# Cached key pages loaded as whole rows and turned in pairs, and the first overflow block gathered between the last scatters, in a decoder step on one core

## What is computed

```python
def _forgetting_attention(q, k, v, fq, fk, q_off):
    ...
        s = jnp.einsum('bqhd,bkhd->bhqk', q[:, a:b], k[:, :nk], ...) * scale
        s = s + fq[...] - fk[...]
        p = jax.nn.softmax(jnp.where(mask, s, -jnp.inf), axis=-1)
        outs.append(jnp.einsum('bhqk,bkhd->bqhd', p, v[:, :nk], ...))
```

## Time and profile before

| | |
|---|---|
| runs | 2081.64, 2071.94, 2058.39 us; median 2071.94 |
| profiled execution | 2073.77 us |
| its span, first to last instruction | 2072.2 us |
| mean granted TensorE clock | 0.939 of full speed |
| PE, PEld, DVE, ACT, POOL busy | 1680.5, 1021.7, 686.2, 310.0, 355.0 us |
| moved by DMA | 674.14 MB, mean 325 GB/s |
| attention groups 0 to 15 | 1165.94 to 1381.07 us of the span |
| overflow block, gather to scatter | 966.73 to 982.72 us |

### The profile page before, as it was taken

One profiled execution on the slowest core, in us unless ns is written; L12 is line 12 of the kernel. 1 busy time (PEld: TensorE's weight loads), 2 busy tenths in 40 slices (PEclk: granted clock), 3 DMA queues, 4 the chain that ended last, 5 costly groups with the idle time before them and its releaser, 6 DMA issues. The chain is left out here.

```text
span 2072.2 us, 34016 instructions
## 1 busy us (share of the span) xinstructions
PE 1680.5 (81%) x13065; PEld 1021.7 (49%) x13066; DVE 686.2 (33%) x1821; ACT 310.0 (15%) x665; POOL 355.0 (17%) x453
## 2 busy tenths in 40 slices
PE   5997989497788987876699988887587889987775
PEld 3455654354455554443455666654354555543432
DVE  0211235611412432221631266547312333331126
ACT  0221211110001111010011244331010011110000
POOL 3000100122211222221001012200122122222210
PEclk8999999699999999997799999998699999999997
DMA  9479883699999999993942599995599999999966
GB/s 334 144 286 339 299 322 102 277 418 422 423 388 380 412 421 409 405 404 145 355 137 81 189 299 333 328 337 195 199 423 423 415 418 406 421 418 407 411 259 228
DMA packets 132060, 674.14 MB, mean 325 GB/s; under 512 B 28111, under 2 KB 40527, under 8 KB 91620
## 3 DMA queue, kind: packets, MB, share of 16 engines
q1 hardware_dynamic: 84880, 570.20, 69.6%
q10 hardware_dynamic: 21604, 55.96, 8.0%
q0 software_dynamic: 25456, 46.27, 6.2%
HBM read 651.03 MB, written 46.94 MB: 337 GB/s over the span
## 5 line engine op out<-in xcount | busy, mean ns | idle before, releaser
L2331 PE MATMUL bank<-ring,work 128*64 128x256 f32 x4096 | 481.8, 388 | 107.1 <-DMA ring<-in_exp_w 104.1
L2331 PEld LDWEIGHTS bank<-ring,work 128*64 128x64 f32 x4096 | 327.4, 140 | 297.7 <-issue 118.5
L2343 PE MATMUL bank<-ring,work 128*64 128x512 f32 x1032 | 251.6, 605 | 63.8 <-DVE work L1768 60.4
L813 POOL DMA_INDIRECT work<-u_d,work x128 | 130.6, 1020 | 781.0 <-DVE work L1736 427.2
L2059 PE MATMUL bank<-ring,uT 128*128 128x512 f32 (+1 forms) x896 | 257.1, 503 | 7.1 <-DVE u L1489 4.2
L1736 DVE COPY work<-work 128x1 int32<-128x1 int32 (+1 forms) x128 | 19.3, 153 | 656.9 <-ACT work L1188 656.1
L2059 PEld LDWEIGHTS bank<-ring,uT 128*128 128x128 f32 (+1 forms) x896 | 119.1, 169 | 136.0 <-issue 114.4
L820 POOL DMA_INDIRECT pair_d<-work x128 | 132.4, 1034 | 124.9 <-issue 73.9
L2343 PEld LDWEIGHTS bank<-ring,work 128*64 128x64 f32 x1032 | 73.9, 136 | 151.7 <-issue 146.6
L1182 ACT COPY work<-bank 128x512 f32<-128x512 f32 x128 | 75.0, 586 | 368.0 <-PE bank L2343 364.6
L1188 ACT ACTIVATE work<-bank 128x128 f32<-128x128 f32 x128 | 35.5, 277 | 531.9 <-PE bank L2331 531.9
(11 more groups left out here) (363 smaller groups left out, 1706.9 us busy)
## 6 DMA issues: line engine op xcount, KB each, us to landing
ring<-in_exp_w SPq DMA_DIRECT2D x128, 2048.0 KB
ring<-in_exp_w SPq DMA_DIRECT2D x128, 1024.0 KB
ring<-in_ada_w SPq DMA_DIRECT2D x24, 2048.0 KB, 12.9
ring<-in_cache_k SPq DMA_DIRECT2D x128, 256.0 KB, 6.4
ring<-in_cache_v SPq DMA_DIRECT2D x128, 256.0 KB, 6.9
ring<-in_gla_w_in SPq DMA_DIRECT2D x6, 2048.0 KB, 15.0
ring<-in_kv_w_mod SPq DMA_DIRECT2D x4, 2048.0 KB, 10.1
work<-pair_d ACTq DMA_DIRECT2D x4, 2048.0 KB, 9.6
```

The costliest lines, as they stand in the source:

```text
L813: pool.indirect_dma_start(out=xg[:, s, :], out_offset=None, in_=u_d, in_offset=bass.IndirectOffsetOnAxis(ap=xi[:, s:s + 1], axis=0), bound ...
L2331: ins = mm(psum[s][64 * c:64 * c + 64, 0:2 * P].rearrange("p (a n) -> p a n", a=2), xT[:, s, j * P + 64 * half:j * P + 64 * half + 64], gu ...
L2343: ins = mm(psum[3 + s][64 * c:64 * c + 64, :], hT[:, s, 64 * f:64 * f + 64], w[:, f, c * 512:(c + 1) * 512], start=(f == 0), stop=(f == 1) ...
```

## The change

Four edits are made together.

1. Keys are loaded as whole rows: one transfer of 128 rows of 4 KB for each page, eight for a sequence instead of sixteen of 2 KB rows, all ahead of its two value halves. Page j is issued when the odd group of the sequence before has turned its page j; both groups of a sequence read the same place, and TensorE waits for a landing only in the even group. Units 6 and 7 belong to pages 4 to 7, both halves.
2. TensorE turns and scores pages two at a time. ScalarE's copy of page 4 moves behind the copies of the turned probabilities, that of page 6 behind the prompt's; VectorE makes the prompt's diagonal ahead of its copy of page 5.
3. The overflow block's gate and up products use the common `gate_up`: 256 columns at a time from the two units where before a loop wrote 128.
4. GpSimd's look-up and gather for overflow block 0 is issued between the scatters of experts 61 and 62; for block j + 1 it is done after block j's results have landed.

The core of the diff:

```diff
-        def key_page(half, j):
-            return ring_pair(4 + 2 * half)[:, j, :]
+        def key_page(j):
+            return ring[:, 4 + j // 2, (j % 2) * D:(j % 2 + 1) * D]
...
-                wr.take(("fox_k", half), 2, (kt_full, 8 * GROUPS - 8 + 8 * half), loads=0)
+                wr.take(("fox_k", half), 2, (kt_full, 8 * GROUPS - 4 + 4 * half), loads=0)
...
+                for j in range(PAGES):
+                    if not first:
+                        sp.wait_ge(kt_full, b * 16 + (j - 7))
+                    elif j % 4 == 0:
+                        free_units(("fox_k", j // 4))
+                    sp.dma_start(key_page(j), W["cache_k"][ds(page[j], 1)].rearrange("o r h d -> (o r) (h d)"))\
+                      .then_inc(sem(f"k_landed{j}"), 16)
                 for half in range(2):
-                    if first:
-                        free_units(("fox_k", half))
-                    for j in range(PAGES):
-                        if not first:
-                            sp.wait_ge(kt_full, b * 16 + (8 * half + j - 15))
-                        rows = W["cache_k"][ds(page[j], 1)].rearrange("o r h d -> (o r) (h d)")
-                        sp.dma_start(key_page(half, j), rows[:, half * 512:(half + 1) * 512])\
-                          .then_inc(sem(f"k_landed{half}{j}"), 16)
                     if first:
                         free_units(("fox_v", half))
...
                 for e in range(60, 64):
                     one(e, e % 3, last=(e >= 61))
+                    if e == 62:
+                        wait(pool, "over_placed", l + 1)
+                        pool.wait_ge(sem("xT_full"), NE * l + NE - 2)
+                        pool.wait_ge(sem("y_stored1"), 16 * Y_STORED[l][1])
+                        gather_over(l, 0)
                 pool.wait_ge(sem("yi_ready"), base + NE)
                 scatter(0, sem("y_stored0"))
...
+            def gather_over(l, j):
                 done = sem(f"pool_over{l}")
+                col = pool.value_load(ov_idx[0:1, ds(j, 1)], min_val=0, max_val=1023)
+                with pool.If(col < 512):
...
                     pool.wait_ge(sem(f"over_stored{l}"), j * 16 + 16)
+                    gather_over(l, j + 1)
...
                 keys_turned(g, 2)
                 if g:
                     exponents(g - 1)
-                keys_turned(g, 4)
                 prompt_exponents(g)
                 if g:
                     probs_turned(g - 1)
+                keys_turned(g, 4)
+                prompt_turned(g)
                 keys_turned(g, 6)
-                prompt_turned(g)
                 prompt_out(g)
...
+                prompt_norm(g)
                 keys_turned(g, 5)
-                prompt_norm(g)
...
+                    gate_up(1, ring[:, 3:5, :].rearrange("p a (k n) -> p k a n", n=FE), done)
...
             def turn_keys(g, j):
                 b, s = divmod(g, 2)
-                pe.wait_ge(sem(f"k_landed{s}{j}"), 16 * (b + 1))
+                if s == 0:
+                    pe.wait_ge(sem(f"k_landed{j}"), 16 * (b + 1))
...
+                turn_keys(g, 3)
                 page_scores(g, 0)
-                turn_keys(g, 3)
                 page_scores(g, 1)
-                turn_keys(g, 4)
-                page_scores(g, 2)
                 new_scores(g)
                 if g:
                     turn_probs(g - 1)
+                turn_keys(g, 4)
                 turn_keys(g, 5)
+                page_scores(g, 2)
                 page_scores(g, 3)
                 prompt_turn(g)
                 turn_keys(g, 6)
+                turn_keys(g, 7)
                 page_scores(g, 4)
-                turn_keys(g, 7)
                 page_scores(g, 5)
```

More of the change, by code:

```diff
@@ L347, in hybrid_trunk_step @@
         sh_down = ln
-        ov_gate, ov_up = (ring[:, n, :].rearrange("p (h m) -> p h m", h=2) for n in (3, 4))
         ov_down = ring[:, 5, :].rearrange("p (f n) -> p f n", f=2)
@@ L849, in experts @@
                     one(e, e % 3, last=(e >= 61))
+                    if e == 62:
[3 more added lines that the diff above has]
+                        gather_over(l, 0)
                 pool.wait_ge(sem("yi_ready"), base + NE)
                 scatter(0, sem("y_stored0"))
-            def overflow(l):
+            def gather_over(l, j):
                 done = sem(f"pool_over{l}")
-                wait(pool, "over_placed", l + 1)
-                pool.wait_ge(sem("xT_full"), NE * l + NE - 2)
-                pool.wait_ge(sem("y_stored1"), 16 * Y_STORED[l][1])
-                def body(j):
+                col = pool.value_load(ov_idx[0:1, ds(j, 1)], min_val=0, max_val=1023)
+                with pool.If(col < 512):
                     col = pool.value_load(ov_idx[0:1, ds(j, 1)], min_val=0, max_val=BLOCKS * NE - 1)
@@ L869, in body, with overflow @@
                         bounds_check=2 * TOK - 1, oob_is_err=False).then_inc(sem(f"over_xg{l}"), 16)
+                    pool.nop()
+                with pool.Else():
+                    pool.nop()
+            def overflow(l):
+                def body(j):
                     pool.wait_ge(sem(f"act_over{l}"), j * 2 + 2)
@@ L2403, in body @@
                     pe.wait_ge(sem(f"over_w{l}"), j * 16 + 16)
-                    for kk in range(KT):
-                        half, jj = divmod(kk, 4)
-                        for c in range(2):
-                            for a, w in enumerate((ov_gate, ov_up)):
-                                ins = mm(psum[1][64 * c:64 * c + 64, a * P:(a + 1) * P],
-                                         xT[:, 1, jj * P + 64 * half:jj * P + 64 * half + 64],
-                                         w.rearrange("p a (k n) -> p (a k) n", n=FE)
-                                         [:, kk, c * P:(c + 1) * P], start=(kk == 0 and a == 0),
-                                         stop=(kk == KT - 1), skip_group_check=True)
-                    ins.then_inc(done, 1)
+                    gate_up(1, ring[:, 3:5, :].rearrange("p a (k n) -> p k a n", n=FE), done)
                     pe.wait_ge(sem(f"over_dve{l}"), j * 3 + 2)
@@ L2545, in turn_keys @@
                     ins = pe.transpose(psum[j % 2][:, i * P:(i + 1) * P],
-                                       key_page(s, j)[:, i * P:(i + 1) * P], ident[:, :])
+                                       key_page(j)[:, (4 * s + i) * P:(4 * s + i + 1) * P], ident[:, :])
                 ins.then_inc(kt_full, 1)
```

## The result

The kernel after takes 2081.46 us (median of 20 runs), the kernel before 2072.61 (20 runs): a ratio of 1.006, 95% interval 1.004 to 1.0081. The change costs about 9 us; the forecast was 2060, and 2081.46 lies at the upper end of its range, on the other side of no change. The profiled execution of the kernel after happened to be one of its short ones, 2065.5 us; at the end of expert 62's down product, ahead of everything that the edits change for TensorE, it is already 8.8 us ahead of the profiled execution of before (940.91 against 949.68). So the comparison is made by stretches, each from its own first row, and a second profile of the kernel after (e12, an execution of 2072.3 us) stands beside the first.

A forecast was written before the change was run, and what follows sets the result against it. The chain to the end bounds: attention stage, output product, overflow block, with transfers and TensorE nearly equal. 4.4 + 2 + 6 = 12.4 gained from 2073.77 or the median 2071.94 gives 2061.4 or 2059.5; predicted 2060, range 2041 to 2082.

The forecast's parts named there:

- Alternation and the order: TensorE, attention stage: turning and scoring pages in twos saves 0.6 us a group; groups 0 to 3 gain 4.4 us.
- The pair of 23.84: Attention stage: two groups without key waits, followed row by row, take 23.84 us in place of 26.15, good to 0.8.
- a round trip: TensorE switching between transposes and scores and back costs about 0.19 to 0.2 us; 3 fewer a group.
- the wait for the diagonal: Attention stage: the 0.82 us wait ahead of the prompt's transposes in a group, claimed to go.
- Keys: Key loads, groups 4 to 15: a pair between 24.4 and 28.3 us, taken as 27.2, as now; no gain.
- The working by landing times: Even groups from group 4: page 7 lands 12.2 us in, is wanted at 7.7, so 4.5 us of wait.
- The pair of 28.3: Attention stage from group 4: an even group of 16.2 us makes the pair 28.3, 1.1 more than now.
- Rival B: Key waits in six even groups lower TensorE's clock: 1.1 + 2.7 us a pair, 12.4 slower, 2086; chance 0.11.
- theory S: Experiments' theory, not the prediction's: with whole-row keys a loop runs in series through SP, landing and even group.
- Output product: Product behind the attention stage: its 2.03 us wait for first weights goes; 2 us gained, bounds 0 and 4.7.
- Overflow: Overflow block, first expert layer: early gather lets TensorE turn rows 6.6 us earlier; 6 gained, bounds 0 and 8.5.
- rival C: Overflow block: the gather is early and brings nothing because something else holds the block, 2066; chance 0.12.

The follow-up runs named there:

- e12: The kernel after, unchanged, run once more for a second profile: 2072.3 us, one run.
- e11: Kernel after with the keys of sequence 0 loaded once and used for all sequences, other key loads left out: 2036.5 us, one run.
- e4: Kernel after with the next sequence's page numbers read early, behind the first value half: 2068.1 us, ratio to before 0.997 to 1.0033.
- e10: e4 with ten places for key pages in place of eight, two pages loaded ahead of the second value half: 2052.0 us, ratio 0.9828 to 0.9931.
- e1: Kernel before with the new order on TensorE, ScalarE and VectorE alone, keys still in halves: 2058.7 us, ratio 0.9912 to 0.9988.
- e2: Kernel before with the whole-row key loads alone, old order on the engines: 2088.9 us, ratio 1.0074 to 1.0139.
- e6: Kernel after with each key page loaded by two transfers of 2 KB rows: 2090.4 us, ratio to before 1.0049 to 1.0112.
- e3: Kernel before with the overflow edits alone (early gather, 256-column gate and up): 2073.4 us, ratio 1.002 (0.9993 to 1.0048).
- e8: e3 with the scatter's index copy put off, so the gather need not wait for expert 61's scatter: 2066.7 us, ratio 0.9973 (0.9935 to 1.001).
- e14: e3 with the 32 KB load in_kv_w_rest issued in the middle of the first expert loop: 2061.5 us, ratio to before 0.9914 to 0.9973.
- e15: Kernel before with the 32 KB load in_kv_w_rest issued in the middle of the first expert loop, nothing else: 2066.8 us, ratio 0.9942 to 0.9999.
- e7: e1 with the page numbers read early, keys in halves: 2050.1 us, ratio to before 0.9881 to 0.9955.
- e9: Kernel before with new order, page numbers read early, keys in halves, and early gather with late scatter index copy: 2059.6 us, ratio 0.9938 (0.9912 to 0.9964).
- e13: e9 with the 32 KB load in_kv_w_rest issued in the middle of the first expert loop: 2044.9 us, ratio to before 0.987 (0.9832 to 0.9908).

## Why the prediction was wrong

- **Alternation and the order: right, and a little low.** The pair of 23.84 by the chain is 23.60 in the trace after and in e11, a round trip 0.27 us where 0.19 to 0.2 was read, and the wait for the diagonal is gone. Groups 0 to 3 take 46.1 us after (a key wait of 0.99 at the end included) and 45.0 in e11, where 47.7 was forecast. They gain more because the 52.14 were not undisturbed: group 0 had the longest wait for the diagonal (1.7) and the lower clock behind it, and goes from 12.68 to 9.40.
- **Keys: the step that failed** is "a pair longer than that leaves the DMA idle, shortens the queue ahead of the next keys, and so shortens the wait again". The DMA did go idle (share 0.90 in the stage after, 0.96 before), and nothing was shortened, because the next keys are not asked for sooner when the DMA is idle: SP stands behind the values product and the page numbers (e4 gives 1.6 us a pair back), and whole-row places come free in odd groups alone (e10 gives 1.9 more). 27.2 was taken between 24.4 and 28.3; it is 29.9 and 30.4, over both bounds. The working by landing times had held: it gave 4.5 us of wait in an even group and none in odd ones, and measured are 27.0 in six even groups, 4.5 each. The pair of 28.3 that came of it was given up for the middle of the two, and what lies beyond it shows on TensorE as busy time at the lower clock, which the forecast put at nothing.
- **Rival B is what was seen**, with a chance of 0.11: key waits in even groups, and the granted clock at 0.50 behind them. Its price was 1.1 + 2.7 a pair; measured against before it is 2.8 a pair. Against e1, which has the same order at a mean clock of 0.98, the kernel after loses 18.8 us in the stage, 9.1 of busy time, which goes with the lower clock (0.92), and 9.7 of waits. I had both halves and put the clock's at little, because the waits are short one by one. That the stage would be 9 us shorter at the full clock is not shown: no run has the waits without the clock, and in e2, at a mean clock of 0.97 and with the slower order, pairs are as long as after. If the loop through the key loads sets their length, as it does in theory S, time won on the clock would have become waits.
- **Rule of the Trainium skill** (DMA: Bandwidth & Descriptors, Specifications): that transfers of 512 B or more run at line rate, by which rows of 4 KB buy nothing over 2 KB. In e6 pairs with 2 KB rows take 30.9, with 4 KB rows 29.9 and 30.4, and twice as many issues are in that difference: the runs lean to the rule, and against the 5% that I read from two stretches.
- **Output product: inside its bounds, but the gain is not shown to be the change's.** 4.5 and 2.1 us were gained on the one trace of before, forecast 2 within 0 and 4.7. But the same stretch takes 9.4, 8.5, 11.5 and 13.0 us in e3, e8, e14 and e15, whose attention and loads are those of before (13.3), and 9.0 to 13.9 in e1, e7, e9 and e13, with keys in halves too. Kernels without the new loads spread over more than what was to be gained.
- **Overflow: the gather was mis-sized and the gain did not carry.** TensorE turned the rows 5.12 us (4.36 in e12) behind expert 63, not 0.9: the landing of scatter 61, which I named as a condition, came late: the look-up that waits for it stands 12.1 us behind its issue (e8, without that wait, turns the rows after 0.87). Of the 3.2 us left at the block's end, the stretch shows 4.0 and 2.9 against the one trace of before, but that trace had a 4.8 us wait of its own; against e1, e2 and e7 (194.2 to 197.2) it is 3 to 7 us longer. So rival C was nearer than the forecast, and with it the sum: the attention stage lost 11 to 13 us where 4.4 were to be gained, and neither of the other two terms is shown to have paid.

## What to carry to other kernels

Wider rows that tie two consumers to one buffer also tie its release to the later of the two: before merging loads, write down when each place comes free, and whether the DMA has anything to load in between. An average of bytes over time says nothing about that. When an early step is moved up on a chain, follow the next loads behind it by name; in e3 and e9 the wait for a 32 KB load in last place of a queue (8.3 and 8.9 us) was longer than what the step had gained (3.1 and 6.8). And where waits are added on TensorE, look at the clock with them: here the busy time grew by as much as the waits (9.1 and 9.7 us against e1). Before a gain in one stretch is booked, see how far that stretch spreads in kernels that don't touch it.

## What the runs showed of the hardware

- The same 32 KB, in rows of 32 B, landed 30.3 (e2), 30.5 (e1), 42.4 (before) and 51.8 us (e3) behind its issue, behind some 10 MB on the same queue and beside 2 MB loads of SP's.
- The scatter of 128 rows lands 2.3 us behind its issue where nothing else moves (the block's own, before); beside the block's 3 MB of weights the look-up that waits for such a landing came 12.1 us behind the issue in the kernel after, 12.7 in e3, and 4.1 in e8, which doesn't wait for it.
- In group 8 of the kernel after TensorE's granted clock falls to 0.50 behind a wait of 1.90 us, stays there through waits of 1.02 and 1.41, and stands at 1.00 again from 1270 on, behind work without a wait from 1265.15. A fall does not follow every such wait: of e1's seven key waits of 1.36 to 1.99 us, those of 1.36, 1.40 and 1.99 have one behind them, those of 1.48, 1.50, 1.65 and 1.81 none. e11, with no key waits, has 1.00 as its mean over the stage.
